# Stick-breaking scores in three passes over split q and k, the strict mask added by VectorE, and one addition moved up at the end

## The reference

```
z = einsum('bqhd,bkhd->bhqk', q * 128**-0.5, k[:, :kl])
mask = kpos < qpos                       # strict
log_keep = where(mask, log_sigmoid(-z), 0)
a = where(mask, exp(z + log_keep + reverse_exclusive_cumsum(log_keep)), 0)
o = einsum('bhqk,bkhd->bqhd', a, v[:, :kl])
```

## Time and profile before

| | |
|---|---|
| median of three runs | 1181.46 us |
| profiled execution, its own time | 1181.35 us |
| its span, first to last instruction | 1179.5 us |
| mean granted TensorE clock | 0.999 |
| TensorE busy in the span | 1166.5 us (99%) |
| VectorE, ScalarE, GpSimd busy in the span | 745.6, 638.7, 681.0 us |
| the 16 units of heads D | about 659.7 to 733.5 us |

### The profile page before, as it was taken

The page is one execution under the profiler, slowest core; times in us unless marked ns, Lnnn a source line. Parts: engine busy times, 40 slices in busy tenths (PEclk is TensorE's granted clock), DMA queues, the critical chain, the costliest instruction groups (busy, mean ns, idle before and its releaser), DMA issues.

```text
span 1179.5 us, 21096 instructions
## 1 busy us (share of the span) xinstructions
PE 1166.5 (99%) x7590; PEld 1073.4 (91%) x7590; DVE 745.6 (63%) x1398; ACT 638.7 (54%) x1003; POOL 681.0 (58%) x593
## 2 busy tenths in 40 slices
PE   8999999999999999999999999999999999999997
PEld 7999999889999999988888889878999999998886
DVE  7888877658787878623251375644878777862325
ACT  6665556548665656533252365444866565653324
POOL 2435555327877777666744332612787777766672
PEclk9999999999999999999999999999999999999999
DMA  7222222112333223223233211311233332323211
GB/s 274 102 107 76 103 73 73 41 67 102 114 107 107 107 104 109 90 107 106 73 106 115 83 72 37 143 37 36 101 114 107 107 107 103 111 90 107 106 73 72
DMA packets 17336, 114.05 MB, mean 97 GB/s; under 512 B 1920, under 2 KB 2304, under 8 KB 4608
## 3 DMA queue, kind: packets, MB, share of 16 engines
q1 hardware_dynamic: 16416, 110.40, 26.1%
q10 hardware_dynamic: 864, 2.88, 0.7%
HBM read 111.18 MB, written 2.10 MB: 96 GB/s over the span
## 4 chain that ended last, share of the span: by engine, by line
PE 93%; DVE 3%; ACT 2%; issue 2%; DMA 0%; DVEq 0%; SPq 0%; ACTq 0%
PE ps L2113 34%; PE ps L2161 17%; PE ps L1914 8%; PE ps L1771 7%; PE ps L1805 3%; PE ps L1833 3%; PE ps L2294 2%; PE ps L2274 2%; PE ps L1878 2%; PE ps L1822 2%; PE ps L1955 2%; PE ps L2198 1%; PE ps L1883 1%; PE ps L1941 1%; PE ps L1713 1%
## 5 line engine op out<-in xcount | busy, mean ns | idle before, releaser
L349 POOL TENSOR_TENSOR w_lo<-w_raw,w_hi 128x512 fp32r<-128x512 f32 (+2 forms) x169 | 256.8, 1550 | 275.8 <-ACT w_hi L473 219.8
L407 POOL TENSOR_TENSOR w_lo<-w_raw,w_hi 128x512 fp32r<-128x512 f32 x120 | 152.8, 1295 | 85.4 <-ACT w_hi L740 66.8
L473 ACT ACTIVATE w_hi<-w_raw 128x2048 fp32r<-128x2048 f32 (+1 forms) x53 | 95.3, 1799 | 166.5 <-PE ps L2161 129.5
L407 POOL TENSOR_TENSOR s_lo<-s_raw,s_hi 128x512 fp32r<-128x512 f32 x120 | 154.7, 1321 | 0.0
L1458 DVE TENSOR_TENSOR hT_lo<-region,hT_hi 128x2048 fp32r<-128x2048 f32 (+1 forms) x22 | 58.9, 2686 | 138.7 <-ACT hT_hi L816 138.7
L2161 PE MATMUL ps<-w_hi,hT_hi 128*128 128x512 f32 x288 | 112.2, 390 | 0.3
L2161 PE MATMUL ps<-w_hi,hT_lo 128*128 128x512 f32 x288 | 112.1, 389 | 0.0
L2161 PE MATMUL ps<-w_lo,hT_hi 128*128 128x512 f32 x288 | 112.1, 389 | 0.0
L740 ACT ACTIVATE w_hi<-w_raw 128x1536 fp32r<-128x1536 f32 x40 | 59.5, 1487 | 71.8 <-PE ps L2113 71.8
L2113 PE MATMUL ps<-hT_hi,w_hi 128*128 128x256 f32 x320 | 90.8, 284 | 0.0
L2113 PE MATMUL ps<-hT_hi,w_lo 128*128 128x256 f32 x320 | 90.6, 283 | 0.0
(11 more groups left out here) (324 smaller groups left out, 3581.3 us busy)
## 6 DMA issues: line engine op xcount, KB each, us to landing
w_raw<-weights SPq DMA_DIRECT2D x99, 1024.0 KB, 4.8
gain<-gains ACTq DMA_DIRECT2D x4, 512.0 KB, 4.2
x<-x_in SPq DMA_DIRECT2D x3, 512.0 KB, 7.4
out<-region SPq DMA_DIRECT2D x3, 512.0 KB, 2.6
w_raw<-weights SPq DMA_DIRECT2D x2, 384.0 KB, 5.6
w_raw<-weights SPq DMA_DIRECT2D x1, 768.0 KB, 8.6
cst<-consts SPq DMA_DIRECT2D x1, 640.0 KB, 10.3
region<-masks SPq DMA_DIRECT2D x1, 576.0 KB, 11.4
```

Of the source, the lines that this page charges most:

```text
L349: ins = pool.tensor_tensor(w_lo[:, slot, cols], w_raw[:, slot, cols], w_hi[:, slot, cols].bitcast(f32), ALU.subtract)
L407: return pool.tensor_tensor(dst, raw, high.bitcast(f32), ALU.subtract)
L473: sc.activation(w_hi[:, slot, 0:used], w_raw[:, slot, 0:used], ACT.Copy).then_inc(w_hi_ready, 1)
```

## The change

Scores of heads D are formed like the other products, by three fp32r passes: q_hi k_hi, q_hi k_lo, q_lo k_hi. ScalarE's query copy writes q_hi, VectorE adds the remainders q_lo (`d_query_low`) and k_lo (in `d_key`). The mask leaves TensorE: VectorE adds it to the last 128 columns of the scores in PSUM (`mask_scores`), and ScalarE's Abs waits for that (`d_masked`) in place of the scores. `mask_scores(n + 1)` stands at the end of VectorE's part of unit n. At the end of the program the addition of the last quarter of tile 3 moves ahead of the scaling of tile 2. One square of the latents writes its unused result to another place.

```diff
             def d_query(h):
-                sc.activation(qk[:, h, :], ps[:, (0, 2, 4, 4)[h], :], ACT.Copy, scale=128 ** -0.5).then_inc(d_q, 1)
+                sc.activation(dq_hi[:, h, :], ps[:, (0, 2, 4, 4)[h], :], ACT.Copy, scale=128 ** -0.5).then_inc(d_qh, 1)
...
-                    sc.wait_ge(d_scores, n + 1)
+                    sc.wait_ge(d_masked, n + 1)
...
             def d_key(h):
-                ve.tensor_copy(dk[:, h, :], ps[:, (1, 3, 5, 5)[h], :]).then_inc(d_k, 1)
+                own.link(ve.tensor_copy(dk_hi[:, h, :], ps[:, (1, 3, 5, 5)[h], :]))
+                ve.tensor_tensor(dk_lo(h), ps[:, (1, 3, 5, 5)[h], :], dk_hi[:, h, :].bitcast(f32), ALU.subtract)\
+                  .then_inc(d_k, 1)
+            def d_query_low(h):
+                ve.wait_ge(d_qh, h + 1)
+                ve.scalar_tensor_tensor(dq_lo[:, h, :], ps[:, (0, 2, 4, 4)[h], :], 128 ** -0.5, dq_hi[:, h, :].bitcast(f32),
+                                        ALU.mult, ALU.subtract).then_inc(d_q, 1)
             for h in range(2):
+                d_query_low(h)
                 d_key(h)
...
+            def mask_scores(n):
+                p, i, m, w = d_unit(n)
+                ve.wait_ge(d_scores, n + 1)
+                diagonal = ps[:, m, w - 128:w]
+                ve.tensor_tensor(diagonal, diagonal, mask_bf[:, M_STRICT:M_STRICT + 128], ALU.add).then_inc(d_masked, 1)
+            mask_scores(0)
             for n in range(16):
...
                 ve.tensor_tensor(sp_, ps[:, m, 0:w], sp_, ALU.subtract).then_inc(d_arg, 1)
+                if n in (2, 5):
+                    d_query_low(2 + n // 5)
                 if n in (3, 6):
                     d_key(1 + n // 3)
...
+                if n < 15:
+                    mask_scores(n + 1)
...
                 add_to_x(W_ALL - 2, t)
-                if t >= 1:
+                if t in (1, 2):
                     scale_back(t - 1)
                 if t == NT - 1:
                     add_last_quarter(W_ALL - 2)
...
+                    scale_back(t - 1)
...
-                pe.matmul(ps[:, m, 0:w], qk[:, 2 * p + m, i * 128:(i + 1) * 128], dk[:, 2 * p + m, 0:w],
-                          start=True, stop=False)
-                pe.matmul(ps[:, m, w - 128:w], ident_bf[:, :], mask_bf[:, M_STRICT:M_STRICT + 128],
-                          start=False, stop=True).then_inc(d_scores, 1)
+                q_hi, q_lo = (q[:, 2 * p + m, i * 128:(i + 1) * 128] for q in (dq_hi, dq_lo))
+                k_hi, k_lo = dk_hi[:, 2 * p + m, 0:w], dk_lo(2 * p + m)[:, 0:w]
+                pe.matmul(ps[:, m, 0:w], q_hi, k_hi, start=True, stop=False)
+                pe.matmul(ps[:, m, 0:w], q_hi, k_lo, start=False, stop=False)
+                pe.matmul(ps[:, m, 0:w], q_lo, k_hi, start=False, stop=True).then_inc(d_scores, 1)
```

More of the change, by code:

```diff
@@ L140, in trunk_program @@
         sin32 = cst[:, C_SIN32:C_SIN32 + 128].rearrange("p (t d) -> p t d", t=NT)
+        dq_hi, dk_hi = (nc.alloc_sbuf_tensor_at(n, [128, 4, SEQ], f32r, offset=o)
+                        for n, o in (("dq_hi", late_at - 4 * 2 * SEQ), ("dk_hi", region_at)))
+        dq_lo = nc.alloc_sbuf_tensor_at("dq_lo", [128, 4, SEQ], f32r, offset=region_at + 4 * 10368)
         masks_f32 = region[:, 12288:12288 + M_END]
@@ L155, in trunk_program, with dk_lo @@
         xn_at, act_end = region_at + 4 * REGION, region_at + 4 * FT * SEQ
+        dk_lows = (at("dk_lo012", [128, 3, SEQ], region_at + 4 * 12416), at("dk_lo3", [128, 1, SEQ], spare_at))
+        def dk_lo(h):
+            return dk_lows[h // 3][:, h % 3, :]
         T_PLACES = ((xn_at, xn_at + 4096), (xn_at + 8192, cst_at + 4 * C_CMUL), (act_end, act_end + 4096))
@@ L210, in trunk_program @@
                              "q_scaled", "kv_scaled", "c_roped"))
-        d_q, d_scores, d_soft, d_sp, d_arg, d_exp, d_turned, d_copied, d_pv, d_out = (
-            sem(n) for n in ("d_q", "d_scores", "d_soft", "d_sp", "d_arg", "d_exp", "d_turned", "d_copied", "d_pv", "d_out"))
+        d_qh, d_q, d_scores, d_masked, d_soft, d_sp, d_arg, d_exp, d_turned, d_copied, d_pv, d_out = (
+            sem(n) for n in ("d_qh", "d_q", "d_scores", "d_masked", "d_soft", "d_sp", "d_arg", "d_exp", "d_turned", "d_copied", "d_pv", "d_out"))
         front_added, front_squared, front_scaled, rstd_ready = (
@@ L922, in square_latent @@
                 else:
-                    sc.activation(v_tok[:, t, 0:256], c_tok[:, t, 384:640], ACT.Square, accum_out=ss[:, j:j + 1])\
+                    sc.activation(q_tok[:, t, 0:256], c_tok[:, t, 384:640], ACT.Square, accum_out=ss[:, j:j + 1])\
                       .then_inc(c_squared, 1)
```

## The result

The changed kernel takes 1190.28 us (median of 4 runs, 1189.67 to 1190.92), the kernel before 1181.49 in the same runs: a ratio of 1.0073, 95% interval 1.006 to 1.0085. It is slower by 8.8 us; 6.4 were forecast. The time lies inside the stated range of 1183.5 to 1192.3, but above the forecast's own 1185.5 to 1190 and at the 1190 of the rival with the falling clock. The profiled execution after took 1189.99, with a span of 1188.1 against 1179.5.

What follows compares the result with a forecast made beforehand. TensorE was taken to bound the kernel (93% of the span). Ring net of TensorE's gain 6.1, collision 0.3 and program end 0 made +6.4 on 1181.35: 1187.8 us, range 1183.5 to 1192.3 (forecast's own 1185.5 to 1190).

Steps and rivals of the forecast that it cites:

- the rival with the falling clock: Unit 10's filler in heads D: TensorE's clock falls after about 4 us of waiting; 1190, up to 1192.3; chance 0.18.
- The ring: Heads D, units 3 to 9: mask, logarithm, three VectorE operations, copies, next mask run without overlap; unit 10's filler +6.5 us.
- The mask's price: VectorE's mask on scores in PSUM: 0.29 plus 0.04 to hand over, 0.33 us; ends 0.25 to 0.46.
- The remainders: VectorE's splits in heads D: query remainder 0.62 us, key split 1.34 in place of 0.60; heads 0 and 1 cost nothing.
- The collision: Running sums of units 5 and 7 beside GpSimd's weight pieces: 0 to 1.03 us each, 0.3 taken for both.
- TensorE's gain: Three passes without mask in heads D: 1.9 us in all, but only 0.38 counted, after unit 10's filler.
- the dearer end: Scores of 128 keys: if a narrow pass cost 0.11 us, they would lose 0.05 a unit, 0.2 in all.
- The end of the program: Last quarter's addition moved: square some 0.4 us earlier, tile 2's transfer about 1 us later; 0 taken, ends -0.4 and +0.4.
- TensorE's pace holds: Rival in heads D: the ring stays within TensorE's unit and only the 1.9 us gain shows, 1179.5 us; chance 0.10.

Runs made afterwards that it cites:

- the pair of copies: Changed kernel plus seven unread VectorE copies in units 2 to 8, directly ahead of the next unit's mask (1194.3 us) or directly behind it (1190.66 us).
- the mask ahead of the copies: Changed kernel with VectorE adding the mask of unit n+1 directly after unit n's difference, ahead of that unit's splits and copies: 1185.36 us, ratio 1.003.
- with the wait filled: Changed kernel plus 15 unread bf16 matmuls of 512 columns on TensorE in unit 10 before the filler: 1187.86 us, ratio 1.0056.
- the mask on VectorE alone: Changed kernel with scores in one float32 matmul again and no splits, keeping the mask on VectorE and the moved addition: 1188.08 us, ratio 1.0054.

## Why the prediction was right, and where it was short

- **The ring** was the right mechanism at nearly the right size. Its turns were put at 4.81, 4.46, 5.45, 6.79, 5.82 and 5.58 and measured 4.78, 4.45, 6.23, 6.76, 5.76 and 5.57. Without the collision in the third (0.86) and the 0.57 of the start the filler is 6.4 later than before, where 6.5 was forecast. The ring took hold one unit earlier than was said, at unit 2's mask (668.28), which makes 0.1 by unit 3's Abs (672.92, less 0.57, against 672.24). And by the prediction's own turns it was slower than TensorE from unit 3 on, not from unit 5: 4.81 against 4.53 (671.99 to 676.52); its sum counted those turns all the same. The waits too came where they were put, half of them at that filler, with 6.8 in all instead of 8 or so. That it is a ring, and not VectorE's load, is what the pair of copies and the mask ahead of the copies showed.
- **The mask's price**, 0.33 with its hand-over, is right: 706.14 to 706.47.
- **The remainders** came to 0.60 and 1.32 beside 0.62 and 1.34. That they cost anything hangs on the mask: with the mask on TensorE they are hidden.
- **The clock** is the step that failed. The prediction counted the wait before unit 10's filler once and left its 24 passes at 4.44, at the full clock; they took 6.05. The fall was a rival of 0.18 that would add 2.2; it came true on top of the forecast, with 1.61 in this trace, and with the wait filled the passes are back at 4.43. The Trainium skill, TensorE: Matmul & The Clock Gate, "Why this matters for your kernels", spoke for it: it asks for no long pauses between bursts of matmuls, since the clock falls back to half. The traces agree for the long waits: TensorE paused for 3.7 us before 711.71 and 1.2 GHz followed. Having forecast a wait of about 4 us, I ought to have put the fall into the forecast. An earlier pause, 2.7 us up to 694.95, was followed by 1.2 GHz too (0.66 in 695 to 700), but TensorE had time to spare there, since the ring set the pace; waits of about that length went both ways (last section). That the median still lies in the range is owed to an upper end that left room for part of this rival.
- **The collision** was a term of 0.3 with an upper end of 2.1. It was 0.86, all at unit 5; unit 7's running sum, which met GpSimd before (2.26), ran at 1.22 in the new order.
- **TensorE's gain** after unit 10 is 0.58, not 0.38. From one score's start to the next, units 11 to 14 gain 0.23, 0.18, 0.20 and -0.02, where 0.16, 0.09, 0.09 and 0.02 were taken. The term that was mis-sized is the mask at 0.06, which costs 0.12 between fp32r passes and 0.11 behind f32 scores (from their start to the filler's second pass 0.93 before, 709.49 to 710.42, and 0.82 with the mask on VectorE alone, 718.22 to 719.04). At 256 keys a pass takes 0.12, not 0.13. Three passes of 128 keys take 0.28, between the 0.26 that was taken and the dearer end.
- **The end of the program** gains 0.24, inside the bounds of 0.4 both ways; nothing was taken.
- **TensorE's pace holds** is refuted as a forecast of this kernel, yet with the mask back on TensorE one gets nearly that: 1180.49 where it said 1179.5.

The terms that were off, 1.6 of clock, 0.56 of collision, -0.24 at the end and -0.2 of TensorE's gain, with the 0.57 by which this execution was late from the start, add up to 2.3; the profiled 1189.99 lies 2.2 over the forecast. The profiled executions come 0.1 to 1.2 us later to heads D than that of the kernel before, and it isn't the splits of heads 0 and 1 ahead of them: with these it was 0.15 in the kernel with copies behind the mask, without them 1.24 in the one with the moved addition alone. What it is stays open.

## What to carry to other kernels

Moving a small step from a full engine to a half-idle one is dear where it makes an engine wait for work that the other does only at the end of its own turn: write down who waits for whom once around, add up the durations, and compare that with the full engine's turn. Busy shares don't show it: VectorE's was 47.32 of 80 us here. Where such a ring can't be avoided, put into it only what the next engine waits for, and all other work behind it, in the shadow of the other engine. Move the step only in those turns in which the full engine's work is longer than the ring, and reckon with two prices of a wait that remains: its own length, and TensorE's clock after it (1.6 to 2.8 us here after waits of 2.8 us and more).

## What the runs showed of the hardware that was not expected

- After waits of TensorE of 2.8, 3.6, 3.7, 3.7 and 4.1 us the next 24 passes of 384 columns took 6.00, 7.22, 6.05, 7.06 and 6.92 us; after waits of at most 0.5 us they took 4.23 to 4.44. So the same wait of 3.7 cost 1.6 in one trace and 2.6 in another: the length of the wait alone doesn't set the length of the slow stretch.
- Nor does it alone decide whether the clock falls. Waits of 2.54 us (copies ahead of the mask), 2.72 (the changed kernel), 2.73 (an unfilled wait of the kernel with matmuls in its later one) and 2.76 (mask ahead of the copies) were followed by 1.2 GHz. One of 2.75, with the copies behind the mask and at nearly the same place as the 2.72, was not: its granted clock stayed at 1.00 where the changed kernel has 0.66. Why, no run here shows.

```profile
694.71 0.94 PE L2391 MATMUL ps<-xn,region 128*128 128x128 f32 x6 [2.75 <-DVE xn L1612]
```
```profile
695.00:700.00 5.00, 4.39 (x28) 3.98 (x27) 3.21 (x5) 2.64 (x5) 2.63 (x2) 1.00 0.25 59
```

- A bf16 matmul of 128 columns between fp32r passes costs 0.12, of which 0.07 shows in the pass behind it.
- A copy from SBUF to SBUF on VectorE takes 0.42 at 128x512 float32, and up to 1.42 and 1.24 where GpSimd's pieces run (at 682.52 in a stretch of pieces from 682.38, at 681.59 in one from 681.26): not only the running sum, which has two inputs in SBUF, is held up. The Trainium skill, SBUF — State Buffer, "Who interferes with whom", names copies in VectorE's two-port modes beside the two-input rule that the prediction used; the prediction gave its line on at most one input without that exception. The trace agrees with the page.
